# Attention's closing product moved into the last block, linear attention opened by token halves, and a stacked low-rank gate

## What is computed

```python
x = x + rmsnorm((silu(gate) * o) @ w_out_b, g_post_b)
h = rms_norm(x, norm_mix)
q, k, v, r, gk_low = split(h @ w_in)              # 4 heads: 128 keys, 256 values; gk_low: 16 wide
log_a = log_sigmoid(gk_low @ w_gk_up + b_gk) / 16  # per key column
# gated linear attention in chunks, decayed by the running sum of log_a
o = rms_norm(o, g_onorm);  x = x + (o * silu(r)) @ w_out
x = x + relu(rms_norm(x) @ w1)**2 @ w2;  return rms_norm(x)
```

## Time and profile before

| | before |
|---|---|
| median of 3 runs | 2657.37 us |
| lowest and highest run | 2654.87, 2657.76 us |
| profiled execution, its own time | 2654.57 us |
| its span | 2652.8 us |
| TensorE busy | 97% |
| VectorE, ScalarE, GpSimd busy | 43%, 33%, 16% |
| closing product, first and last matmul | 1342.6 and 1443.5 us |
| first value projection | 1496.5 us |

### The profile page before, as it was taken

How to read it: one execution, slowest core, us unless ns; L and a number is a source line. 1 busy time by engine, 2 the same in 40 slices (tenths; PEclk the granted TensorE clock), 3 DMA queues, 4 the chain that set the end, 5 groups by cost and what they waited for, 6 DMA issues and landing times. The chain is left out here.

```text
span 2652.8 us, 36049 instructions
## 1 busy us (share of the span) xinstructions
PE 2576.4 (97%) x13200; PEld 2186.5 (82%) x13200; DVE 1144.7 (43%) x2219; ACT 863.8 (33%) x1569; POOL 424.2 (16%) x892
## 2 busy tenths in 40 slices
PE   8999999999999999999878999999999999999999
PEld 7888888888887987788766788888888888888887
DVE  4333333323423410677744576666343333333334
ACT  5222222222313423555433444443331221112212
POOL 4444444443000305000001011011000000000000
PEclk9999999999999999999989999999999999999999
DMA  6211111110533221211143201111431111111111
GB/s 236 74 50 47 60 49 49 53 68 27 201 112 96 72 92 46 58 58 58 48 161 114 64 28 45 57 56 56 157 135 48 56 51 37 53 49 55 40 48 72
DMA packets 72629, 194.77 MB, mean 73 GB/s; under 512 B 8080, under 2 KB 28752, under 8 KB 71760
## 3 DMA queue, kind: packets, MB, share of 16 engines
q1 hardware_dynamic: 72528, 193.41, 21.9%
HBM read 152.48 MB, written 36.70 MB: 71 GB/s over the span
## 5 line engine op out<-in xcount | busy, mean ns | idle before, releaser
L1066 PE MATMUL ra_qkv_ps<-ra_wh,ra_xl 128*128 (+1 forms) x512 | 207.0, 404 | 11.6 <-DVE ra_wl L901 9.3
L1066 PE MATMUL ra_qkv_ps<-ra_wh,ra_xh 128*128 (+1 forms) x512 | 201.3, 393 | 0.0
L1066 PE MATMUL ra_qkv_ps<-ra_wl,ra_xh 128*128 (+1 forms) x512 | 200.7, 392 | 0.0
L3198 PE MATMUL wc_g_ps<-x_upper,ff_w1l 128*128 128x512 f32 x512 | 199.3, 389 | 0.0
L3198 PE MATMUL wc_g_ps<-x_upper,ff_w1h 128*128 128x512 f32 x512 | 199.2, 389 | 0.0
L3214 PE MATMUL wc_y_ps<-ff_w2h,ff_hl 128*128 128x512 f32 x512 | 199.2, 389 | 0.0
L3214 PE MATMUL wc_y_ps<-ff_w2l,ff_hh 128*128 128x512 f32 x512 | 199.2, 389 | 0.0
L3198 PE MATMUL wc_g_ps<-x_lower,ff_w1h 128*128 128x512 f32 x512 | 199.2, 389 | 0.0
L3214 PE MATMUL wc_y_ps<-ff_w2h,ff_hh 128*128 128x512 f32 x512 | 199.2, 389 | 0.0
L3152 DVE TENSOR_TENSOR ff_acc<-wc_y_ps,ff_acc 128x1024 f32<-128x1024 f32 x63 | 77.2, 1225 | 210.8 <-PE wc_y_ps L3214 210.8
L3077 ACT ACTIVATE ff_relu<-wc_g_ps 128x512 f32<-128x512 f32 x64 | 38.3, 598 | 379.1 <-PE wc_g_ps L3198 379.1
(11 more groups left out here) (404 smaller groups left out, 6470.6 us busy)
## 6 DMA issues: line engine op xcount, KB each, us to landing
staging<-in_w_ff SPq DMA_DIRECT2D x64, 512.0 KB, 3.8
ra_raw<-in_w_in_a SPq DMA_DIRECT2D x30, 768.0 KB, 4.6
gated_a<-ra_sg SPq DMA_DIRECT2D x64, 128.0 KB, 1.9
staging<-in_w_vr_c SPq DMA_DIRECT2D x16, 512.0 KB, 3.9
wa_gin<-gated_a SPq DMA_DIRECT2D x6, 1024.0 KB, 4.8
staging<-in_w_out_a SPq DMA_DIRECT2D x9, 512.0 KB, 3.9
staging<-in_x_cols SPq DMA_DIRECT2D x8, 512.0 KB, 5.2
ra_opening<-in_x SPq DMA_DIRECT2D x8, 512.0 KB, 7.5
```

The lines of the kernel that those rows point to most:

```text
L1066: last = pe.matmul(out, a[:, kt, t * P:(t + 1) * P], b[:, ds(slot, 1), kt, at:at + n].rearrange("p a n -> p (a n)"), start=(kt == 0 and i ...
L3198: last = pe.matmul(f_ps[j % 2][:, :], a[kt // 2][:, kt % 2, f * P:(f + 1) * P], b[:, kt, half * HALF:(half + 1) * HALF], start=(kt == 0 an ...
```

## The change

`close_mixer` is removed. A new `attention_closing` gives the same product as part of the last block, unrolled over its 8 tiles. Its transposes run one tile behind: tile 0 is transposed inside tile 2 (behind kt 2 and 3), and each tile t - 1 inside tile t (behind kt 6 and 7). Token tile 0 arrives in one transfer and not in two. In between its tiles each engine does early work of the linear attention (the functions named `early`): the gate weight, the first upward weight and the first two weight pieces of q and k, and DMAs of two more. The transposes of tile 7 (`wb.split`) stand in `gla_heads`.

The linear attention's opening is cut by token halves: with tiles 0 to 3 TensorE projects the gate and q before tile 7 is transposed, then k of the first half, then the second half.

The low-rank gate is stacked. The 16 columns of its weight are laid out six times, four times as upper and two times as lower part, so that a product with `x_upper` has 96 rows of output and one with `x_lower` 64: 16 matmuls a half. The 96 rows, each as an upper or a lower part by a table of 0 and -1 (`parts`), meet a 96-row upward weight of upper and lower parts in a single fp32r matmul. Buffers are placed anew; the closing of the linear attention and the feed-forward keep their work and order.

```diff
+    out["gla_parts"] = np.repeat(np.array([[0, 0], [-1, 0], [0, -1], [-1, -1], [0, 0], [-1, 0]], f), GRANK, axis=0)
...
-def close_mixer(nc, tag, gated, w, gain, x, g_post, ident, neghalf, staging, arrived, ahead, x_next,
...
-    return lay(qk), lay(vr), np.ascontiguousarray(w[:, :, 2 * k + 2 * v:].transpose(1, 0, 2))
+    return lay(qk), lay(vr), np.ascontiguousarray(np.tile(w[:, :, 2 * k + 2 * v:], (1, 1, 6)).transpose(1, 0, 2))
...
+    low_w = place("gl_low_w", [P, KT, LOW], F32R, 124 * KB)
...
+        load_piece(0, 4)
+        load_piece(0, 5)
...
+    def sync_early(sp, t):
+        if t == 0:
+            for dst, src in ((up_raw, w_up[:, 0:GK]), (bias, b_gk), (mask, masks), (parts, which)):
+                sp.dma_start(dst[:], src).then_inc(con_in, 16)
+            sp.wait_ge(wb.wl_done, KT - 1)
+            sp.dma_start(raw_low, w_low).then_inc(low_in, 16)
+            sp.wait_ge(wb.wl_done, KT)
+            sp.dma_start(raw[:, 1, :], w_qk[0, :, 4:8, :].rearrange("p k n -> p (k n)")).then_inc(raw_in[1], 16)
+        if t == 2:
+            sp.wait_ge(low_w_done, 1)
+            sp.dma_start(raw[:, 0, :], w_qk[0, :, 0:4, :].rearrange("p k n -> p (k n)")).then_inc(raw_in[0], 16)
+        if t in (4, 5):
+            sp.wait_ge(wl_done, t - 3)
+            sp.dma_start(raw[:, t % 2, :], w_vr[0, :, 2 * t - 8:2 * t - 6, :].rearrange("p k n -> p (k n)"))\
+              .then_inc(raw_in[t % 2], 16)
...
+    def scalar_early(act, t):
+        if t == 2:
+            act.wait_ge(low_gained, 1)
+            act.activation(low_w[:, :, 0:4 * GRANK], raw_low[:, :, 0:4 * GRANK], ACT.Copy).then_inc(low_w_high, 1)
+            up_upper(act, 0)
+        if t in (4, 5):
+            piece_upper(act, 0, t - 4)
...
+        act.wait_ge(wb.y_done, NT)
+        low_copy(0)
+        qk_copy(0, 0)
         for half in range(2):
-            act.wait_ge(low_mm, half + 1)
-            act.activation(low[:, half * HALF:(half + 1) * HALF], vr_ps[half][0:GRANK, :], ACT.Copy).then_inc(low_copied, 1)
+            wb.split[0](act, half=half)
+        log_gates(0, 0)
+        act.wait_ge(wb.y_mm, NT)
         w_upper(0, 2)
-        log_gates(0)
         w_upper(0, 3)
-        qk_copy(0, 0)
+        qk_copy(0, 1)
...
         w_upper(0, 5)
+        low_copy(1)
+        exponentials(0, 0)
         qk_copy(0, 2)
-        exponentials(0, 0)
+        log_gates(0, 1)
         qk_copy(0, 3)
...
+    def vector_early(dve, t):
+        if t == 1:
+            dve.wait_ge(low_in, 16)
+            dve.tensor_tensor(raw_low, raw_low, gain[:, :].unsqueeze(2).broadcast_to([P, KT, LOW]), ALU.mult)\
+               .then_inc(low_gained, 1)
+        if t == 2:
+            dve.wait_ge(low_w_high, 1)
+            dve.tensor_tensor(low_w[:, :, 4 * GRANK:LOW], raw_low[:, :, 4 * GRANK:LOW],
+                              low_w[:, :, 0:2 * GRANK].bitcast(F32), ALU.subtract).then_inc(low_w_done, 1)
+            dve.wait_ge(con_in, 64)
+            up_lower(dve, 0)
+        if t in (4, 5):
+            piece_lower(dve, 0, t - 4)
...
+        low_rest(0)
+        wb.split[1](dve)
         dve.wait_ge(ones_set, 1)
-        split_gates(0, True)
+        split_gates(0, 0)
+        for half in range(2):
+            wb.split[2](dve, half=half)
+        sum_gates(0, 0)
         w_lower(0, 2)
-        sum_gates(0)
         w_lower(0, 3)
+        for slot in range(2):
+            dve.wait_ge(wb.x_out[slot], 16 * NT // 2)
         exponents(0, 0, 0)
+        low_rest(1)
         w_lower(0, 4)
         w_lower(0, 5)
+        split_gates(0, 1)
         products(0, 0)
+        sum_gates(0, 1)
...
+        def project_low(half):
+            at = slice(half * HALF, (half + 1) * HALF)
+            pe.wait_ge(wb.xl_done, NT * (half + 1))
+            for r in range(KT):
+                if r:
+                    pe.matmul(vr_ps[half][0:4 * GRANK, :], low_w[:, r - 1, 0:4 * GRANK], xl[:, r - 1, at], start=False, stop=False)
+                if r < KT - 1:
+                    pe.matmul(vr_ps[half][0:LOW, :], low_w[:, r, :], xh[:, r, at], start=(r == 0), stop=False)
+            pe.matmul(vr_ps[half][0:4 * GRANK, :], low_w[:, KT - 1, 0:4 * GRANK], xl[:, KT - 1, at], start=False, stop=False)
+            pe.matmul(vr_ps[half][0:LOW, :], low_w[:, KT - 1, :], xh[:, KT - 1, at], start=False, stop=True).then_inc(low_mm, 1)
+
+        def gates(h, only=None):
+            if only is None:
+                pe.wait_ge(up_done, h + 1)
+            else:
+                pe.wait_ge(low_done, only + 1)
+            for half in (range(2) if only is None else (only,)):
+                last = pe.matmul(gate_bank(half, only is not None), up[:, :], low[:, half * HALF:(half + 1) * HALF],
+                                 start=True, stop=True)
             last.then_inc(z_mm, 1)
...
-        pe.wait_ge(lowl_done, 1)
+        pe.wait_ge(low_w_done, 1)
+        project_low(0)
+        pe.wait_ge(wl_done, 2)
+        pe.wait_ge(wb.y_done, NT - 1)
+        project_qk(0, 0)
+        gates(0, 0)
         for half in range(2):
-            transposed_product(vr_ps[half][0:GRANK, :], lowh, lowl, slice(0, GRANK), half).then_inc(low_mm, 1)
-        pe.wait_ge(low_copied, 2)
-        gates(0, True)
-        project_qk(0, 0)
+            wb.split[3](pe, half=half)
+        project_qk(0, 1)
+        project_low(1)
+        project_qk(0, 2)
+        gates(0, 1)
+        project_qk(0, 3)
...
+    def load_g(sp, t):
+        src = gated[:, t * P:(t + 1) * P].rearrange("(k p) n -> p k n", p=P)
+        if t >= 2:
+            sp.wait_ge(gl_done, 2 * (1 if t == 2 else t))
+        sp.dma_start(g_place(t)[:, :, :], src).then_inc(g1_in if t == 1 else g_in, 16)
+
+    def load_res(sp, t):
+        if t < 2:
+            sp.wait_ge(gl_done, 4)
+        else:
+            sp.wait_ge(y_done, t - 1)
+        sp.dma_start(xin[:, t % 2, :], x[t * P:(t + 1) * P, :]).then_inc(res_in[t % 2], 16)
+
+    def sync(sp, later):
+        load_g(sp, 0)
+        load_g(sp, 1)
+        for kt in range(2, KW):
+            sp.wait_ge(wl_done, kt - 1)
+            sp.dma_start(staging[:, kt % 2, :], w[kt * P:(kt + 1) * P, :]).then_inc(raw_in[kt % 2], 16)
+            if kt == 3:
+                load_g(sp, 2)
+        sp.dma_start(post[:], g_post.partition_broadcast(P)).then_inc(post_in, 16)
+        load_res(sp, 0)
+        load_res(sp, 1)
+        for t in range(NT):
+            if t + 3 < NT:
+                load_g(sp, t + 3)
+            later(sp, t)
+            sp.wait_ge(y_done, t + 1)
+            sp.dma_start(x_next[t * P:(t + 1) * P, :], y[:, t % 2, :]).then_inc(x_out[t % 2], 16)
+            if t + 2 < NT:
+                load_res(sp, t + 2)
...
+    def scalar(act, later):
+        for half in range(2):
+            g_upper(act, 0, half)
+        w_upper(act, 0)
+        w_upper(act, 1)
+        for half in range(2):
+            g_upper(act, 1, half)
+        for kt in range(2, KW):
+            w_upper(act, kt)
+        for t in range(1, NT):
+            square_y(act, t - 1)
+            if t >= 2:
+                for half in range(2):
+                    x_upper(act, t - 2, half)
+            if t + 1 < NT:
+                for half in range(2):
+                    g_upper(act, t + 1, half)
+            square_x(act, t - 1)
+            later(act, t)
+        square_y(act, NT - 1)
+        for half in range(2):
+            x_upper(act, NT - 2, half)
+        square_x(act, NT - 1)
...
+    def vector(dve, later):
+        for half in range(2):
+            g_lower(dve, 0, half)
+        w_lower(dve, 0)
+        w_lower(dve, 1)
+        for half in range(2):
+            g_lower(dve, 1, half)
+        for kt in range(2, KW):
+            w_lower(dve, kt)
+        for t in range(1, NT):
+            if t >= 2:
+                for half in range(2):
+                    x_lower(dve, t - 2, half)
+            finish(dve, t - 1)
+            if t + 1 < NT:
+                for half in range(2):
+                    g_lower(dve, t + 1, half)
+            scale_x(dve, t - 1)
+            later(dve, t)
+        for half in range(2):
+            x_lower(dve, NT - 2, half)
+        finish(dve, NT - 1)
...
+    def tensor(pe):
+        for kt in range(KW):
+            for t in range(2):
+                multiply(pe, t, kt)
+        for t in range(2, NT):
+            for kt in range(KW):
+                multiply(pe, t, kt)
+                if t == 2 and kt in (2, 3):
+                    transpose_x(pe, 0, kt - 2)
+                if kt >= KW - 2:
+                    transpose_x(pe, t - 1, kt - (KW - 2))
...
-        close_mixer(nc, "wb_", gated_b, t["w_out_b"], None, x1, t["g_post_b"], ident, neghalf, staging, arrived["close_b"],
-                    loads("gla", [pieces(t["w_qk_c"], i, 4) for i in range(2)]), x2, feature_major=True, xT=xT)
...
+            wb.programs[0](sp, early[0])
...
-        "w_gk_up": i["l0_w_gk_up_2"], "b_gk": columns(i["l0_b_gk_2"]),
```

(48 more changed lines are left out.)

719 lines of the change are left out of this document (250 added, 469 removed).

## The result

The changed kernel takes **2636.84 us** (median of four runs, 2636.08 to 2638.51), the kernel before 2657.57 beside it (2654.87 to 2658.16): 0.9925 of the time, 95% interval 0.9908 to 0.9942. The forecast was 2636. By the medians 20.7 us are gone. The profiled execution took 2637.07 us, with a span of 2635.3; 17.5 us of span are gone, where the sum said 19.5.

The account below looks back on a forecast made before the run. TensorE, busy 97%, was taken as the bound. Minus 20.3, minus 4.4, plus 3.1, plus 1.5, plus 0.6 is minus 19.5 us: 2635.1 from 2654.6, taken as 2636 between two bases; own range 2631 to 2641.

Parts of the forecast that it names:

- Term 1: From tile 7's end to the first value projection: fewer gate matmuls and covered waits, 31.8 against 52.6 us, minus 20.3 net.
- Rival F: Second stacked product's chain: one more table-load switch adds a drain, 1.4 us longer, total 2637.4; chance 0.1.
- Term 2: Heads 1 to 3: a stacked fp32r product replaces each float32 gate pair, 1.46 us each, minus 4.4 in all.
- Term 3: Tile 2 of the closing product: a new TensorE wait, plus 3.1 us, and a lower clock behind it, plus 1.5.
- Term 4: The start: token tile 0 arrives in one piece, so all behind is later, plus 0.6 us.
- Term 5: Linear attention's closing and the feed-forward keep their lists: no difference, between minus 1 and plus 1 us.
- A: No loss in tile 2: the new wait and its clock cost don't come, about 2631 us; chance 0.13.
- B: Tiles 3 to 7 all wait, their 1 us margin used up by handovers: 2641 to 2655 us; chance 0.12.
- C: Heads don't get shorter because VectorE becomes the bound: 4.4 us stay, 2640 us; chance 0.07.
- D: Opening by halves fails: tile 7's transposes still wait for `wb_xn`, up to 5.9 us, total 2642; chance 0.08.
- E: Slower: a late token tile transfer lengthens each closing-product tile, about 2674 us; chance 0.03.

Follow-up runs that it names:

- e7: The changed kernel with tile 7 transposed before the first half's gate rows and q, undoing the opening by halves alone; 2646.9 us.
- e0: The changed kernel measured once more, with no edit; 2637.38 us.
- e4: The changed kernel with ScalarE copying the second half's gate rows before the upper parts of pieces 4 and 5; 2632.0 us.
- e6: The changed kernel with the stacked products of heads 1 to 3 in plain float32; 2641.4 us.
- e3: The changed kernel with the gate weight's transfer started earlier and, in tile 2, tile 1's finish ahead of tile 0's lower parts; 2631.4 us.
- e10: The changed kernel with the transposes in tiles 3 to 7 of the closing product two rows (12 matmuls) earlier; 2645.1 us.
- e5: The changed kernel with token tile 0 loaded in two halves, each with its own semaphore; 2635.2 us.
- e9: The changed kernel with eight more matmuls with the gate weight's upper part in each half's projection; 2636.7 us.
- e1: The changed kernel with the gate weight's transfer started earlier, the lists of ScalarE and VectorE unchanged; 2634.7 us.
- e8: The changed kernel with early gate weight transfer, new order in tile 2, early gate-row copy and token tile 0 in halves; 2627.84 us.

## Why the prediction was right

**Term 1, the opening, minus 20.3.** From tile 7's end (1450.85) to the first value projection (1483.86) it took 33.0 us, forecast 31.8. Every cover held: TensorE reached the first stacked product and tile 7's transposes with no wait, and e7 shows what that was worth. Of the 1.2 us that were missed, 0.7 are the second stacked product's wait, 1.9 and not 1.2. The timeline of ScalarE shows where it arose:

```profile
1462.94 0.63 ACT L1997 ACTIVATE gl_mn<-gl_mn 128x512 f32<-128x512 f32 x1 [0.72 <-DVE gl_mn L2149]
1463.59 1.28 ACT L1999 ACT_TABLE_LOAD   x1
1464.88 0.63 ACT L1999 ACTIVATE gl_mn<-gl_mn 128x512 f32<-128x512 f32 x1
...
1475.42 1.33 ACT L1974 ACTIVATE gl_vrh<-staging,gains 128x512 fp32r<-128x512 f32 x2 [1.08 <-DMA staging<-in_w_vr_c]
1476.66 0.57 ACT L1992 ACTIVATE gl_low_high<-gl_vr_ps 96x512 fp32r<-96x512 f32 x1
```

VectorE's last lower part ahead of the transfer:

```profile
1467.56 2.72 DVE L2110 SCALAR_TENSOR_TENSOR gl_vrl<-staging,gains,gl_vrh 128x512 fp32r<-128x512 f32 x4
```

It ends at 1470.28, 19.4 us behind tile 7's end, to the tenth as forecast. But ScalarE gets the last piece 5.1 later and not 4.0 later: the step that was short is this transfer, priced from one row, where here two pieces of 512 KB are on their way together. So the rows came 1.1 later than forecast, and TensorE 0.5 later (0.15 of it because the working's own terms up to this product add up to 24.95 and not to 24.8). The 1.9 is also the longest such wait of this order: in the eight profiles with the opening of the change the piece came 4.4 to 5.1 us behind that lower part, and the wait was 1.1 to 1.9 (1.5 in e0). The 1.2 of the forecast lies inside that; 4.0 was too short for all of them. That the copy's place behind that piece was what held it, as the working had it, e4 shows. Rival F would have put 1.4 between the load and the Ln or ahead of the load. The load ends at 1464.87 and Ln begins at 1464.88, and the load begins 0.02 behind the Exp's end. The Trainium skill ("ScalarE: Activation LUTs", "What ACT_TABLE_LOAD costs") has a drain of 1.38 beside the load; the trace doesn't agree in this place.

**Term 2, the heads, minus 4.4.** R fell by 4.9; e6 puts back 3.9 in R and 4.5 in the median. Right, and on the path as argued. The 4.9 has two clock losses in it (last section): some 1.7 of the kernel before in the heads, and 1.4 of the change behind them. 4.9 less 1.7 plus 1.4 is 4.6; for the 0.7 between that and e6's 3.9 there is no run.

**Term 3, tile 2, plus 3.1 and 1.5.** Measured 3.4 (2.7 to 3.6 in the nine profiles with this tile 2), and in the profile of the change 1.7 for the clock (C of the change less C of e3 is 5.1). Both stated reasons were true, and they were in a row: either alone, put right, brought 1 us of the wait at most. The sentence "even a punctual weight doesn't help" was nearly right: it brought the finish 0.5 forward, for in the change VectorE did wait for the weight (5.67 us, ahead of L2117) and made both lower parts behind it. The weight was issued at 1375.59 and took 4.8, forecast 1374 and 4.4; since tile 2 itself began 1.5 later than in the kernel before, only 0.5 of the landing time is an error. The claim that tiles 3 to 7 are covered "by about 1 us" was a little short: 1.4, as e10's section shows.

**Term 4, the start, plus 0.6.** 0.9 (S, 11.7 to 12.6), and e5 takes it back.

**Term 5, the rest, 0.** The lists were unchanged, yet up to 1.4 us came from the clock.

**The sum** as measured: minus 19.6 in O, minus 4.9 in R, plus 5.5 in C (the wait, the clock and tile 6's transposes), plus 0.9 in S, minus 0.1 between S and C. That is minus 18.2; the profile of the change was 0.7 later when the attention stage ended, so its span is 17.5 shorter. The sum said 19.5. That the forecast came within 0.8 of the median is in part luck: the sum was 1.3 too large against these two profiles, the medians fell by 20.7, and the base was chosen between profiled execution and median. The rivals: A needed the order to be harmless (e3 shows the cost that was there), B needed the cover of 1.4 us to be used up, C is refuted by e6, D by the profile, which has no wait ahead of tile 7's transposes (e7 shows what it would have cost), and of E's long transfers nothing was seen: no wait for a token tile beyond the 4.2 us at tile 2's start, which were there before.

## What to carry to other kernels

When a step is moved into another program, write each engine's list in the order of the new place and ask what stands ahead of the longest handover chain there: in tile 2 two harmless-looking items each held the chain, and undoing one alone took away less than a third of the wait, undoing both all of it. Transposes and other work that needs only early tiles are worth as much as cover as any saved instruction (10 us here). A saving in front of a chain that is fixed on another engine comes back as a wait: of two times eight matmuls saved only the first eight counted, as long as ScalarE's list stayed as it was (e9), and with its copy moved forward the wait was gone (e4).

## What the hardware showed unexpectedly

**The same wait has not always the same price in clock.** Behind the new wait in tile 2 the granted clock fell in nine profiles of eleven. C less that wait lay between 73.0 (e1) and 76.0 (e9), e10 left out, whose other tiles wait too, against 72.7 in e3: 0.3 to 3.3 us, a part of which, in e5, e6 and e9, is a longer stretch at the lower level behind the 4.2 us wait that opens tile 2. The two rows are the change, behind 3.4 us of waiting, and e1, behind 2.7.

```profile
1388.07:1392.50 4.43, 4.43 (x17) 3.67 (x18) 0.54 (x2) 1.60 (x4) 0.32 (x2) 0.61 0.94 322
```

```profile
1387.30:1391.70 4.40, 4.40 (x24) 3.72 (x25) 1.23 (x4) 2.32 (x5) 0.74 (x2) 1.00 0.94 333
```

In the same time 17 matmuls or 24. It isn't length alone: e4 waited 3.2 and kept its clock, e5 2.7 and lost it.

**Far behind, work that nobody touched differs by 1.4 us.** Ahead of the linear attention's closing product TensorE waits 2.0 us in every kernel. Behind it the clock fell in nine of thirteen profiles (the change and its variants), and not in those of e0, e4, e8 and e9, nor before. R is 1151.4 to 1151.5 or 1149.8 to 1150.0 accordingly (e6, with its float32 products, 1155.3). The five us behind that wait's end, of the change and then of e0:

```profile
1838.37:1843.36 4.99, 4.99 (x15) 4.01 (x16) 0.54 (x2) 0.51 (x2) 0.00 (x0) 0.66 0.00 0
```

```profile
1839.67:1844.66 4.99, 4.99 (x22) 4.18 (x23) 0.94 (x3) 0.90 (x3) 0.74 (x2) 1.00 0.19 53
```

And the kernel before shows a fall with no wait at all. In the heads, TensorE busy for 10.00 of 10.00 us:

```profile
1625.00:1635.00 10.00, 10.00 (x36) 7.41 (x35) 8.24 (x27) 6.27 (x12) 4.10 (x2) 0.83 0.04 13
```

0.83 over 10 us is a loss of 1.7. The slow matmuls begin some 3 us behind the start of a head's float32 gate products, but e6, which has three such pairs, shows no fall in its heads, and neither does any other variant. So the cause stays open. All this is a part of the spread of 2 to 8 us between the executions of one kernel, and the reason why effects of 1 us were read from marks here and not from totals.
